# Latent attention's two norms taken out of their own stage and folded into evictions, keys, values and softmax

## The reference, cut to what matters

```python
def rmsnorm(x, g):
    xf = x.astype(jnp.float32)
    y = xf * lax.rsqrt(jnp.mean(xf * xf, axis=-1, keepdims=True) + NORM_EPS)
    return (y * g.astype(jnp.float32)).astype(x.dtype)

cq = heads(rmsnorm(pc_q, c_g_q) @ c_w_uq, C_HEADS, C_NOPE + C_ROPE)   # pc_q: 512 features
ckv = rmsnorm(pc_kv, c_g_kv)                                          # pc_kv: 256 features
'c_kn': heads(ckv @ c_w_uk, C_HEADS, C_NOPE)      # keys, 4 heads x 128
'c_v': heads(ckv @ c_w_uv, C_HEADS, C_VD)         # values, 4 heads x 128
score = (einsum(qn, kn) + einsum(qr, kr)) * (C_NOPE + C_ROPE) ** -0.5   # kr isn't normed
p = joint_softmax([score over latent keys, score over context keys])
```

## Time and profile before

| | |
|---|---|
| median of 3 runs | 3573.71 us (3572.57 to 3575.56) |
| the profiled execution, its own time | 3579.07 us |
| its span | 3576.7 us |
| TensorE busy, weight loads busy | 3231.0 us (90%), 2907.9 us (81%) |
| VectorE, ScalarE, GpSimd busy | 1709.5 us (48%), 1071.7 us (30%), 413.8 us (12%) |
| mean DMA rate | 85 GB/s |

### The profile page before, as it was taken

One profiled execution on the slowest core, in us unless ns is written; L12 is line 12 of the kernel. 1 busy time (PEld: TensorE's weight loads), 2 busy tenths in 40 slices (PEclk: granted clock), 3 DMA queues, 4 the chain that ended last, 5 costly groups with the idle time before them and its releaser, 6 DMA issues. The chain is left out here.

```text
span 3576.7 us, 46251 instructions
## 1 busy us (share of the span) xinstructions
PE 3231.0 (90%) x17984; PEld 2907.9 (81%) x17984; DVE 1709.5 (48%) x3152; ACT 1071.7 (30%) x1788; POOL 413.8 (12%) x286
## 2 busy tenths in 40 slices
PE   5999999979999988699999959999979999869997
PEld 5989988968898788599999948877867787657875
DVE  6644345423347755764211375545433477443334
ACT  2223334323323432211211222434333324322221
POOL 0001100100021010321022020020100110121011
PEclk6999999989999999799999979999989999989998
DMA  5411220311052113342221233141320431322322
GB/s 193 159 39 54 77 89 25 118 31 42 24 183 71 36 60 118 118 118 76 71 70 44 86 130 97 60 118 36 107 59 24 147 95 36 129 94 79 103 83 100
DMA packets 332307, 303.76 MB, mean 85 GB/s; under 512 B 39822, under 2 KB 309852, under 8 KB 330204
## 3 DMA queue, kind: packets, MB, share of 16 engines
q1 hardware_dynamic: 315406, 229.74, 21.3%
q10 hardware_dynamic: 16718, 71.52, 5.3%
HBM read 266.47 MB, written 34.34 MB: 84 GB/s over the span
## 5 line engine op out<-in xcount | busy, mean ns | idle before, releaser
L754 PE MATMUL ps<-u_hi,w_hi 128*128 128x384 f32 (+1 forms) x2352 | 685.3, 353 | 44.6 <-issue 12.4
L754 PE MATMUL ps<-u_lo,w_hi 128*128 128x384 f32 (+1 forms) x2352 | 680.1, 351 | 0.0
L754 PE MATMUL ps<-u_hi,w_lo 128*128 128x384 f32 (+1 forms) x2352 | 679.0, 350 | 0.0
L1574 DVE TENSOR_TENSOR w_lo<-w_raw,w_hi 128x2048 fp32r<-128x2048 f32 x145 | 354.8, 2447 | 463.7 <-ACT w_hi L1163 461.5
L754 PEld LDWEIGHTS ps<-u_hi,w_hi 128*128 128x128 f32 x2352 | 431.7, 190 | 79.0 <-issue 47.5
L754 PEld LDWEIGHTS ps<-u_lo,w_hi 128*128 128x128 f32 x2352 | 434.7, 190 | 22.0
L754 PEld LDWEIGHTS ps<-u_hi,w_lo 128*128 128x128 f32 x2352 | 433.9, 190 | 22.5
L1163 ACT ACTIVATE w_hi<-w_raw 128x2048 fp32r<-128x2048 f32 x145 | 277.3, 1913 | 521.5 <-PE ps L754 285.2
L848 PE MATMUL ps<-u_hi,w_hi 128*128 128x384 f32 (+1 forms) x816 | 311.9, 382 | 4.5 <-ACT space L1307 3.5
L848 PE MATMUL ps<-u_hi,w_lo 128*128 128x384 f32 (+1 forms) x816 | 297.8, 365 | 0.0
L848 PE MATMUL ps<-u_lo,w_hi 128*128 128x384 f32 (+1 forms) x816 | 294.7, 361 | 0.0
(11 more groups left out here) (237 smaller groups left out, 4534.2 us busy)
## 6 DMA issues: line engine op xcount, KB each, us to landing
w_raw<-in_w_in SPq DMA_DIRECT2D x288, 256.0 KB, 4.0
space<-in_w_mod SPq DMA_DIRECT2D x48, 1024.0 KB, 5.5
w_raw<-in_w_gate_up SPq DMA_DIRECT2D x176, 256.0 KB, 3.9
w_raw<-in_w_down SPq DMA_DIRECT2D x96, 192.0 KB, 2.8
w_raw<-in_w_branch SPq DMA_DIRECT2D x64, 256.0 KB, 3.4
h_scratch<-space ACTq DMA_DIRECT2D x4, 3072.0 KB, 9.8
space<-h_scratch ACTq DMA_DIRECT2D x4, 3072.0 KB, 10.3
m_scratch<-space ACTq DMA_DIRECT2D x3, 3072.0 KB, 10.0
```

The costliest lines, as they stand in the source:

```text
L754: last = nc.tensor.matmul(ps[:, 2 * (t % 2) + b, 0:a1 - a0], wv[w][:, k, j * P:(j + 1) * P], xx[:, k, a0:a1], start=(k == 0 and w == 0 and ...
L1574: V.tensor_tensor(w_lo[slot][:, :], w_raw[slot][:, :], w_hi[slot][:, :].bitcast(F32), ALU.subtract).then_inc(w_lo_done, 1)
```

## The change

The stage `norm_c` goes. The gain is applied when c_kv and c_q are evicted; the root of the mean square, which is a number for each token, is applied later. ScalarE evicts a tile twice: the high part (copy, scaled by the gain) and its square. VectorE then makes the low part out of PSUM and releases the accumulator, and adds the squares. The sums over partitions are one-column products between tiles on TensorE (c_kv's after c_q's first tile, c_q's after uq_nope's first tile), with a mean on VectorE and a power on GpSimd. c_kv's roots are spread over the partitions by products with a broadcast weight after c_q's third tile and copied to tile 27. The keys' tiles of ukv are evicted by VectorE, multiplied by tile 27; the values get their root as the scale of ScalarE's copy after the transpose; the queries' root goes into the scale of the exponential and of the negated maximum. As the gemm of c_q is now followed by that of uq, TensorE's uq_nope waits chunk by chunk for c_q's low parts, in its first tile.

```diff
-        gemm(Group(l, "c_kv", 1, 2, KD, False, "u", "copy", 12), Group(l, "c_q", 2, 2, KD, q, "u", "copy", 8))
-        phases.append(("norm_c", l, None))
+        gemm(Group(l, "c_kv", 1, 2, KD, False, "u", "latent", 0), Group(l, "c_q", 2, 2, KD, q, "u", "latent", 2))
...
+        C_SQ, C_RSTD = (8, 9, 10, 11, 26, 24), 27
...
                         for k in range(g.kc):
+                            if g.name == "uq_nope" and j == 0:
+                                made = g.t0 - HEADS + k
+                                pe.wait_ge(acc_free[made % 2], made // 2 + 1)
                             chunk_product(g, slot, t, j, k)
+                    if g.name == "c_q" and t == g.t0:
+                        latent_sums(g.layer, 0)
+                    if g.name == "c_q" and t == g.t0 + 2:
+                        latent_spread(g.layer)
+                    if g.name == "uq_nope" and j == 0:
+                        latent_sums(g.layer, 1)
...
+            def latent_sums(l, i):
+                pe.wait_ge(c_total, 2 * l + i + 1)
+                if i or l:
+                    pe.wait_ge(c_mean_ready, 2 * l + i)
+                for t in range(CT if i and l == DEPTH - 1 else 0, NT):
+                    last = nc.tensor.matmul(ps[:, 4, t:t + 1], space[:, C_SQ[2 * i], t * P:(t + 1) * P],
+                                            ones[:, 0:1], start=True, stop=True)
+                last.then_inc(c_sums, 1)
+            def latent_spread(l):
+                pe.wait_ge(c_root_ready, 2 * l + 1)
+                if l:
+                    pe.wait_ge(c_rstd, l)
+                for t in range(NT):
+                    at = t % 3 * P
+                    last = nc.tensor.matmul(ps[:, 6 + t // 3, at:at + P], c_root[:, 0, t:t + 1].to_broadcast([P, P]),
+                                            ident[:, :], start=True, stop=True)
+                last.then_inc(c_spread, 1)
...
+                    elif g.kind == "latent":
+                        act.wait_ge(acc_ready, t + 1)
+                        at = t - g.t0 + g.dst
+                        _, c_gain, hi, _ = latent(g, at)
+                        A(two(hi, g.lat), acc(t % 2, g.lat), ACT.Copy, scale=c_gain)
+                        A(tile_at(C_SQ[at], g.lat), acc(t % 2, g.lat), ACT.Square).then_inc(c_split, 1)
+                    elif g.name == "ukv" and j < HEADS:
+                        pass
...
+                    if g.name == "uq_nope":
+                        act.wait_ge(c_spread, l + 1)
+                        A(tile_at(C_RSTD, False), ps[:, 6:8, 0:TOK // 2], ACT.Copy).then_inc(c_rstd, 1)
...
-                          scale=SCALE[kind], accum_out=den[:, n.map % 4:n.map % 4 + 1]).then_inc(probs_ready, 1)
+                          scale=c_scale[:, t:t + 1] if kind == "c" else SCALE[kind], accum_out=den[:, n.map % 4:n.map % 4 + 1]).then_inc(probs_ready, 1)
...
-                            A(v_tok[:, t, :], bank, ACT.Copy).then_inc(tr_copied, 1)
+                            A(v_tok[:, t, :], bank, ACT.Copy,
+                              scale=c_root[:, 0, t:t + 1] if kind == "prep_c" else 1.0).then_inc(tr_copied, 1)
...
+                    if g.name == "uq_nope" and j == 0:
+                        latent_mean(g.layer, 1)
+                        dve.wait_ge(c_root_ready, 2 * g.layer + 2)
+                        own.did(V.tensor_scalar(c_scale[:, :], c_root[:, 1], SCALE["c"], None, ALU.mult))
+                        own.did(V.tensor_scalar(c_neg[:, :], c_root[:, 1], -SCALE["c"], None, ALU.mult))
+                        own.wait()
...
+                    elif g.kind == "latent":
+                        at = t - g.t0 + g.dst
+                        k, c_gain, hi, lo = latent(g, at)
+                        dve.wait_ge(c_split, 6 * g.layer + at + 1)
+                        V.scalar_tensor_tensor(two(lo, g.lat), acc(t % 2, g.lat), c_gain, two(hi, g.lat).bitcast(F32),
+                                               ALU.mult, ALU.subtract).then_inc(acc_free[t % 2], 1)
+                        if k:
+                            total = space[:, C_SQ[g.dst], toks(g.lat)]
+                            own.wait()
+                            own.did(V.tensor_tensor(total, total, space[:, C_SQ[at], toks(g.lat)], ALU.add))
+                        if k == g.n * g.nt - 1:
+                            own.wait()
+                            dve.sem_inc(c_total, 1)
+                        if g.name == "c_q" and k == 0:
+                            latent_mean(g.layer, 0)
+                    elif g.name == "ukv" and j < HEADS:
+                        dve.wait_ge(c_rstd, g.layer + 1)
+                        dve.wait_ge(acc_ready, t + 1)
+                        V.tensor_tensor(tile_at(g.dst[j], False), tile_at(C_RSTD, False), acc(t % 2, False),
+                                        ALU.mult).then_inc(acc_free[t % 2], 1)
...
-                            V.tensor_scalar(nmx[:, c4:c4 + 1], mx[:, c4:c4 + 1], -SCALE[kind], None,
+                            V.tensor_scalar(nmx[:, c4:c4 + 1], mx[:, c4:c4 + 1],
+                                            c_neg[:, t:t + 1] if kind == "c" else -SCALE[kind], None,
...
+                    if g.name in ("c_kv", "uq_nope"):
+                        i = int(g.name == "uq_nope")
+                        pool.wait_ge(c_mean_ready, 2 * g.layer + i + 1)
+                        G.tensor_tensor(c_root[:, i], c_mean[:, i], half_neg[:, 0:1].to_broadcast([P, NT]),
+                                        ALU.pow).then_inc(c_root_ready, 1)
```

More of the change, by code:

```diff
@@ L1250, in squares @@
                 tok = toks(lat)
-                if not squared_before(kind, l):
-                    for k in range(chunks):
-                        square(k, scr, lat, chunk_at(src[k], lat), chunk_at)
                 n.sq += chunks - 1
@@ L1264, in squares @@
                     return
-                if kind != "norm_c":
-                    split(following, 0, 0)
+                split(following, 0, 0)
                 hi, _ = dst
@@ L1271, in squares @@
                     tmp = space[:, scr[3 + k % 2], :]
-                    if shift is None:
-                        A(hi[:, k, tok], tmp[:, tok], ACT.Copy).then_inc(split_hi, 1)
-                    else:
-                        for sg, seg in segments(lat):
-                            last = A(hi[:, k, seg], tmp[:, seg], ACT.Identity, bias=shift(k, sg))
-                        last.then_inc(split_hi, 1)
+                    for sg, seg in segments(lat):
+                        last = A(hi[:, k, seg], tmp[:, seg], ACT.Identity, bias=shift(k, sg))
+                    last.then_inc(split_hi, 1)
                     n.chunk += 1
@@ L1614, in gemm_unit, with latent_mean @@
                         dve.sem_inc(acc_free[t % 2], 1)
+            def latent_mean(l, i):
+                t0 = CT if i and l == DEPTH - 1 else 0
+                dve.wait_ge(c_sums, 2 * l + i + 1)
+                V.tensor_scalar(c_mean[:, i, t0:], ps[:, 4, t0:NT], 1.0 / ((4 if i else 2) * P), EPS, ALU.mult,
+                                ALU.add).then_inc(c_mean_ready, 1)
             def scalars():
@@ L1682, in norm @@
                 t0 = CT if lat else 0
-                for k in range(0 if squared_before(kind, l) else chunks):
-                    add_square(k, scr, lat)
                 n.sq += chunks - 1
@@ L1715, in low @@
                     tmp, (hi, lo) = space[:, scr[3 + k % 2], :], dst
-                    if shift is None:
-                        last = V.tensor_tensor(lo[:, k, tok], tmp[:, tok], hi[:, k, tok].bitcast(F32), ALU.subtract)
-                    else:
-                        for sg, seg in segments(lat):
-                            last = V.scalar_tensor_tensor(lo[:, k, seg], tmp[:, seg], shift(k, sg),
-                                                          hi[:, k, seg].bitcast(F32), ALU.add, ALU.subtract)
+                    for sg, seg in segments(lat):
+                        last = V.scalar_tensor_tensor(lo[:, k, seg], tmp[:, seg], shift(k, sg),
+                                                      hi[:, k, seg].bitcast(F32), ALU.add, ALU.subtract)
                     last.then_inc(u_ready, 1)
@@ L2239, in _ @@
                     own.did(G.memset(mean[:, :], 1.0))
+                    own.did(G.memset(c_mean[:, :, :], 1.0))
                     own.wait()
```

28 lines of the change are left out of this document (15 added, 13 removed).

## The result

The changed kernel takes **3523.15 us** in the median of 4 runs (3520.36 to 3525.05), the kernel before 3574.64 in the same comparison (3572.57 to 3578.7): a ratio of 0.985, 95% interval 0.9835 to 0.9866. The forecast was 3518.4 with a range of 3510 to 3532. The profiled execution lasted 3524.54 us (forecast 3523.8) with a span of 3522.6, against 3579.07 and 3576.7 before, 54.5 less.

A forecast was written before the change was run, and what follows sets the result against it. Time was taken to go mainly where TensorE stands still or runs at half clock; 72.1 us removed less 16.8 added gave 55.3, off the 3573.71 median 3518.4 us, range 3510 to 3532.

The forecast's parts named there:

- a clock under 1.00 after ukv's stall: Sign of being wrong: TensorE's granted clock falling below full speed after the 2.7 us stall forecast in ukv.
- The hole: Between c_q and uq_nope, around the removed norm: 39.36 us in layer 0 and 32.73 in layer 1 go, together 72.1.
- the seams: At c_q to uq, the hand-over between gemm phases adds 0.4 us a layer on TensorE, 0.8 in all.
- Nobody waits at the seam: c_q to uq_nope: TensorE's waits at chunk 3, sums and tile 2 are 0; chunk 3 bounded at 1 us a layer.
- Rival A: The seam leaks: VectorE or ScalarE late at thin places, 5 to 10 us, 3523 to 3528; chance 0.14.
- Sums: Sums of squares moved into TensorE's stream: three sets at 1.8 us and one at 1.2 add 6.6 us.
- Spreads: Spreading the roots by six broadcast-weight products adds 1.2 us a layer, 2.4 in all; 4.8 at half clock.
- ukv: Key evictions on VectorE wait behind the gates' weight split: TensorE stalls 2.7 us a layer, 5.4 in all.
- Rival B: Clock falls inside the new stream, two to four drops, 6 to 12 us, 3524 to 3530; chance 0.12.
- Values: Six ScalarE copies a layer after the transposes take a pointer scale at 0.09 us each, 1.1 in all.
- Softmax: Branch c's exponential and negated maximum take pointers; 6.0 us if all on the path, 0.5 taken because of fill products.
- Rival C: TensorE waits at the seam for the other engines: 15 us dearer, 3533; chance 0.05.

The follow-up runs named there:

- no_roots: Changed kernel without the latents' sums, spreads, means, powers and roots, ScalarE evicting the keys again, values and softmax with constant scales; 3509.99 us, ratio 0.9807.
- const_softmax: Changed kernel with constants again for the exponential's scale and the negated maximum in branch c, leaving out the queries' roots; 3529.81 us, ratio 0.9865.
- after_again: The changed kernel unaltered, run again for its scatter; 3527.99 us, ratio 0.9858 to the kernel before.
- before_more_code: Kernel before, with the six sums of layer 1's first latent norm issued twice; 3579.55 us against 3575.82, ratio 1.0008.
- sums_twice: Changed kernel with every latent sum of squares and every spread product issued twice; 3534.46 us, ratio 0.9883.
- keys_first: Changed kernel with VectorE evicting ukv's first two key tiles ahead of the gates' weight split, made in two pieces behind tiles 1 and 2; 3521.2 us, ratio 0.9832.
- after: The changed kernel itself, as first profiled, against the kernel before; 3523.15 us, ratio 0.985.
- barrier: Changed kernel with TensorE waiting for the other engines between c_q and uq; 3534.26 us, ratio 0.9869.
- before_dve_keys: Kernel before, with VectorE instead of ScalarE evicting ukv's four key tiles by plain copy behind the gates' weight split; 3587.13 us, ratio 1.0024.

## Why the prediction was right, and where it was off

**Right in the mechanism and in the sum.** The two stretches gained 55.4 us where 55.3 was worked out. That agreement is partly luck, since terms went either way: sums and spreads were put 1.2 us too high and the values 0.7, ukv 1.5 too low. One of the prediction's signs of being wrong did appear, a clock under 1.00 after ukv's stall, in layer 1. Term by term:

- *The hole*, 72.1 forecast. P gained 63.25, and by no_roots 7.8 of new products lie in it, with 0.8 for the seams (not measured apart): 71.9. Right.
- *Nobody waits at the seam* (chunk 3, sums, tile 2 in layer 1, thin covers of 0.2 to 0.6 us): no wait in either layer, with 0.4 to 1.0 us to spare at chunk 3 and the sums. The copy that makes the high part took 0.90 in place of the 0.81 assumed, for it is scaled by a pointer too; the cover bore it. Rival A did not come about.
- *Sums*, 6.6 forecast, 3 x 1.26 + 0.80 = 4.6 from start to next start. The duration was taken from a window in the hole at low clock; in that profile's records 12 sums lasted 1.77 us at a clock of 0.77 and 2.72 at 0.50, while in the new stream at 1.00 they last 1.39 and take 1.26 to the next start. *Spreads*, 2.4 forecast, 2.5 measured. Together 7.1 by the rows and 7.8 by no_roots, against 9.0.
- *ukv*, 5.4 forecast. The waits are 2.51 + 2.30 = 4.8. Left out of the sum was the clock after them, 1.7 us in layer 1; taking the wait away gives back 6.9. The step that failed is the one that priced the stall at its length alone. Rival B had the mechanism, but with two to four falls at 3.1 and 2.6 us each. There was one, and it cost 1.7 (1.6 to 2.3 in the experiments).
- *Values*, 1.1 forecast, 0.4 measured (no_roots and const_softmax together): most of the 12 copies were covered.
- *Softmax*, 0.5 forecast, 0.5 measured. The Trainium skill, ScalarE: Activation LUTs, section What ACT_TABLE_LOAD costs, says that a pointer operand adds about 93 ns; the traces agree (88 and 89 ns). What it would have made of the time, 3.7 us, was not paid: const_softmax gives 0.5 back for both pointers.
- *Rival C*, 15 us dearer: built, it was 9.2 by the stretches and 6.3 by the medians.

**The last 4.7 us.** The median is 3523.15, not 3518.4. The kernel before accounts for 0.9 of it: its median was 3573.71 where the prediction started and 3574.64 beside the changed kernel. The gain was 51.5 us by these medians, 52.0 beside after_again, and 54.5 between the two profiled executions, so 0.8 to 3.8 of the 55.3 are missing. 2.2 to 3.5 us went in branch d of layer 1, which no step of the prediction looked at: the shorter code before it moved a code fetch into a full burst of transfers. before_more_code shows that such a shift is enough for it; that it is the whole cause in the changed kernel is not shown. No kernel made from it has the burst free of fetches. Two have the 16 KB fetch ahead of the burst and an 8 KB one inside: there the weight's split starts at 43.49 (sums_twice) and 43.83 (no_roots) in place of 44.05, against 43.00 in the kernel before, and D still lasts 257.71 and 255.70. What remains, up to 1.6 us, is within what the runs of one kernel differ by.

## What to carry to other kernels

Follow each moved eviction to the engine that takes it over and read what that engine has in front of it: here four evictions behind a 2.3 us weight split cost 6.9 us, and putting the first two ahead of it (the split in two pieces behind them) gave all of that back. A stage of a serial chain can be removed almost at its full length if every link finds room beside products, even when the covers are tenths of a microsecond, provided that their durations come from rows. For terms of a few microseconds compare stretches between fixed marks, since whole runs scatter by more.

## What the runs showed of the hardware that I had not expected

- **Code placement reaches far.** 24 more TensorE instructions made an untouched stage, whose loss lies more than 200 us later, 2.5 us longer. The 16 KB fetch had moved into a burst of weights on the same DMA engines. The Trainium skill, Runtime: NRT & Kernel Launch, section Instruction fetch mechanics, says that an engine's code is refilled in 16 KiB blocks and that crossing one is mostly hidden. The page after has 122 fetches of 2.00 MB in all on this queue, which agrees in size; in this one, beside a burst, a weight came 1.0 us later and a wait grew from 1.77 to 2.81 us.
- **The clock can fall with TensorE never idle**: three of three sets of 24 one-column sum records, 2.60 us each, were followed by a stretch at 0.57 to 0.71, while the latents' sets of 12 and 16, and 24 records of 128 columns, were not. The set alone does not decide: branch d's own 16 one-column records in layer 0 (L743), with sparse transposes behind them, were followed by 0.64 and 0.51 in keys_first and by 1.00 in after.
- **A given idle time doesn't decide alone.** After waits of 2.3 us in layer 1's ukv it fell in all six profiles that had them, after 2.5 us in layer 0 it fell in one (barrier) and not in five (after, after_again, const_softmax, before_dve_keys, sums_twice); 2.79 us at barrier's seam in layer 1 left it at 1.00, and 3.75 in layer 0 did not. What the engine did in the microseconds before differs between these places; what of it decides was not tried.
